# A 64-column product of zeros ahead of feed-forward stretches on TensorE

## The reference, cut to what matters

```
y = jnp.square(jax.nn.relu(h @ ff_w_in[layer])) @ ff_w_out[layer]      # layers 0 and 1: 1024 -> 4096 -> 1024
u, gate = jnp.split(h @ w_up, 2, axis=-1)                              # third: 1024 -> 2 x 2816
u = dwconv_grid(u, w_cf, b_cf, rows, width)
return (jax.nn.silu(u) * gate) @ w_down                                # 2816 -> 1024
```

## Time and profile before

| what | value |
|---|---|
| median of 3 runs | 1011.76 us (1010.94 to 1012.22) |
| the profiled execution, its own time | 1011.14 us |
| its span (first to last instruction) | 1009.2 us, so 1.9 us lie around it |
| TensorE matmuls, busy | 983.7 us, 97% of the span |
| TensorE weight loads, busy (beside the matmuls) | 865.8 us, 86% |
| VectorE, ScalarE, GpSimd busy | 801.6, 539.9, 77.4 us |
| DMA | 243.60 MB, mean 241 GB/s |
| mean granted TensorE clock | 0.996 of full speed |

### The profile page before, as it was taken

The page is one execution under the profiler, slowest core; times in us unless marked ns, Lnnn a source line. Parts: engine busy times, 40 slices in busy tenths (PEclk is TensorE's granted clock), DMA queues, the critical chain, the costliest instruction groups (busy, mean ns, idle before and its releaser), DMA issues.

```text
span 1009.2 us, 16926 instructions
## 1 busy us (share of the span) xinstructions
PE 983.7 (97%) x6900; PEld 865.8 (86%) x6901; DVE 801.6 (79%) x1208; ACT 539.9 (53%) x706; POOL 77.4 (8%) x80
## 2 busy tenths in 40 slices
PE   6999999999999999999999999999999999999997
PEld 3687799989987989887889999988998889999996
DVE  2449799858988988877979778873799789888896
ACT  4354554444446547775545455464765765454544
POOL 0000000000000000000540000000791000000000
PEclk9999999999999999999999999999999999999999
DMA  9999699969997999002998877735433386555511
GB/s 340 387 384 375 224 337 393 349 225 358 351 338 255 287 365 353 2 2 84 377 372 299 282 269 286 255 95 167 127 132 127 119 282 220 186 189 190 186 43 42
DMA packets 130332, 243.60 MB, mean 241 GB/s; under 512 B 6586, under 2 KB 95311, under 8 KB 124111
## 3 DMA queue, kind: packets, MB, share of 16 engines
q1 hardware_dynamic: 125616, 238.77, 66.9%
q10 hardware_dynamic: 4639, 3.76, 1.4%
HBM read 239.37 MB, written 1.05 MB: 238 GB/s over the span
## 4 chain that ended last, share of the span: by engine, by line
PE 76%; DVE 6%; DMA 5%; POOL 4%; ACT 4%; SPq 2%; issue 2%; POOLq 0%; DVEq 0%; ACTq 0%
PE bank L2039 26%; PE bank L1971 11%; PE bank L1973 11%; PE bank L1972 11%; PE bank L2051 3%; DMA raw<-in_a_w_in_dram 3%; DVE wlo L1199 2%; DMA raw<-in_cmp_w_dram 1%; PE bank L2324 1%; PE bank L2350 1%; SPq L654 1%; DMA raw<-in_b_w_in_dram 1%; ACT whi L724 1%; PE bank L1865 1%; PE bank L2362 1%
## 5 line engine op out<-in xcount | busy, mean ns | idle before, releaser
L1199 DVE TENSOR_TENSOR wlo<-raw,whi 128x2048 fp32r<-128x2048 f32 x143 | 327.3, 2295 | 47.3 <-ACT whi L724 46.2
L724 ACT ACTIVATE whi<-raw 128x2048 fp32r<-128x2048 f32 x144 | 274.3, 1905 | 144.6 <-PE bank L2039 76.6
L1971 PE MATMUL bank<-hcat,whi 128*128 128x256 f32 x1096 | 309.1, 282 | 2.3 <-DVE wlo L1199 1.9
L1972 PE MATMUL bank<-hcat,whi 128*128 128x256 f32 x1096 | 307.0, 280 | 0.0
L1973 PE MATMUL bank<-hcat,wlo 128*128 128x256 f32 x1096 | 306.9, 280 | 0.0
L1971 PEld LDWEIGHTS bank<-hcat,whi 128*128 128x128 f32 x1096 | 206.0, 188 | 9.1 <-issue 3.5
L1973 PEld LDWEIGHTS bank<-hcat,wlo 128*128 128x128 f32 x1096 | 208.9, 191 | 0.0
L1972 PEld LDWEIGHTS bank<-hcat,whi 128*128 128x128 f32 x1096 | 206.0, 188 | 1.4
L1818 DVE SCALAR_TENSOR_TENSOR cvt<-ut,vec,cvt 128x189 f32<-128x189 f32 (+2 forms) x176 | 68.2, 429 | 19.3 <-ACT cvt L1162 16.8
L2039 PE MATMUL bank<-whi,fhi 128*128 128x512 f32 x240 | 74.7, 392 | 0.0
L2039 PE MATMUL bank<-wlo,fhi 128*128 128x512 f32 x240 | 74.0, 390 | 0.0
(11 more groups left out here) (432 smaller groups left out, 1649.6 us busy)
## 6 DMA issues: line engine op xcount, KB each, us to landing
raw<-in_ada_w_dram SPq DMA_DIRECT2D x40, 1024.0 KB, 8.5
raw<-in_ff_w_in_dram SPq DMA_DIRECT2D x32, 1024.0 KB, 7.9
raw<-in_ff_w_out_dram SPq DMA_DIRECT2D x32, 1024.0 KB, 7.3
raw<-in_w_ada_dram SPq DMA_DIRECT2D x24, 1024.0 KB, 6.3
raw<-in_w_up_dram SPq DMA_DIRECT2D x22, 1024.0 KB, 5.1
raw<-in_w_in_dram SPq DMA_DIRECT2D x12, 1024.0 KB, 5.5
raw<-in_w_down_dram SPq DMA_DIRECT2D x11, 1024.0 KB, 4.9
raw<-in_ada_w_dram SPq DMA_DIRECT2D x16, 512.0 KB, 12.0
```

The lines of the kernel that those rows point to most:

```text
L724: act.activation(whi[:, m % SPL, 0:w], raw[:, pl.nm[m] % RAW, 0:w], ACT.Copy).then_inc(s_hi, 1)
L1199: dve.tensor_tensor(wlo[:, m % SPL, 0:w], raw[:, pl.nm[m] % RAW, 0:w], whi[:, m % SPL, 0:w], ALU.subtract).then_inc(s_lo, 1)
L1971: pe.matmul(dst, wh[:, kt, n], ah[:, kt, :], start=kt == 0, stop=False)
L1972: pe.matmul(dst, wh[:, kt, n], al[:, kt, :], start=False, stop=False)
```

## The change

A function `offset_start` issues one more matmul, of bf16 zeros: stationary `zb[:, 0:128]`, moving `zb[:, 0:64]`, into the first 64 columns of the bank that the stretch behind it writes, with `start` and `stop` set. The first product of the stretch begins with `start=True` too and so overwrites it. It is issued behind the waits of the stretch and ahead of its 48 products, for each `ff_in(c)` with c > 0 (15 in each of the first two layers) and for `up(M_UP[c + 1])` (10 in the third layer). `up(M_GA[...])`, which follows `up(M_UP[...])`, gets none, nor does any stretch outside of the feed-forward layers.

```diff
+KICK = 64
...
-            def feature_major(m, bank, ah, al, between=None):
+            def offset_start(bank):
+                pe.matmul(bank[:, 0:KICK], zb[:, 0:P], zb[:, 0:KICK], start=True, stop=True)
+
+            def feature_major(m, bank, ah, al, between=None, offset=False):
                 wh, wl = w_of(m)
+                if offset:
+                    offset_start(bank)
                 for nt in range(wh.shape[2] // P):
...
-            def linear_mid(m, ah, al, tm=False, o=None, between=None):
+            def linear_mid(m, ah, al, tm=False, o=None, between=None, offset=False):
...
-                    mm = feature_major(m, bank, ah, al, between)
+                    mm = feature_major(m, bank, ah, al, between, offset)
...
-                    linear_mid(m0 + (2 * c - 1 if c else 0), hh, hl, o=o)
+                    linear_mid(m0 + (2 * c - 1 if c else 0), hh, hl, o=o, offset=c > 0)
...
-                def up(m, bank, o=None):
+                def up(m, bank, o=None, offset=False):
                     split_ready(m)
                     if o is None:
-                        feature_major(m, ps[bank], hh, hl).then_inc(s_mm, 1)
+                        feature_major(m, ps[bank], hh, hl, offset=offset).then_inc(s_mm, 1)
...
-                        up(M_UP[c + 1], 6 + (c + 1) % 2)
+                        up(M_UP[c + 1], 6 + (c + 1) % 2, offset=True)
```

## The result

The changed kernel takes 1016.83 us in the median of 4 runs (1015.06 to 1018.0) against 1011.37 for the one before in the same session (1010.94 to 1012.22): a ratio of 1.0053, 95% interval 1.004 to 1.0066. It is slower. The profiled execution took 1015.06 us, the fastest of the four, with a span of 1013.2.

What follows compares the result with a forecast made beforehand. TensorE's matmul chain was taken as the bound. Pace gain 10.5 us, less 4.4 for kicks and 0.6 for settling, gives 5.5 less than the 1011.76 median: 1006.3 us, with an 8-in-10 range of 1004.8 to 1016.8.

Steps and rivals of the forecast that it cites:

- The bound: Feed-forward layers: TensorE's matmuls fill the windows, so the distance from one product to the next is their time.
- The two paces and their worth: Feature-major stretches of 48 products: 117.7 or 113.3 ns a product, 0.21 us a stretch, 10.5 us for 50 stretches.
- full flip: All 50 feed-forward stretches move to the fast pace: 5.5 us less after costs, 1006.3 us, chance 0.47.
- The no-flip rival: Kicked stretches stay at 117.7 ns, so the kicks are pure cost: 4.4 us more, 1016.2 us, chance 0.32.
- Whether it does: At the kicked stretches: whether the kick moves them to the fast pace, bounded by 0 and 10.5 us gained.
- The 17 pauses: Feature-major starts behind a pause of 0.15 us or more in the earlier trace: 14 fast, 3 slow.
- The six starts without a gap: Feature-major starts right behind short products, with no pause, in the earlier trace: all 6 slow.
- All or nothing: Kicked stretches: the same outcome expected nearly everywhere, because every 512-column run ends in the same steady rhythm.
- The price: On TensorE's chain, each kick costs a whole weight load, 0.11 us, 4.4 us for 40; bounds 1.1 to 5.2.
- the 229 ns a product of the rival: 512-column runs slow from 226.7 to 229 ns a product as the pace flips: 2.4 us lost, 1008.7, chance 0.06.
- Settling: At starts of fast stretches, a few slower products: some 0.016 us a start, 0.6 us for 40.
- The lower price: Kicks at the 25 ns issue floor: 1.0 us for 40, ending near 1002.9; cheaper kicks got chance 0.02.

Runs made afterwards that it cites:

- e13: Changed kernel with the last 512-column product of each run issued as 448 and 64 columns instead of a kick there, bf16 kick kept at five other places: 1005.16 us.
- e2: Changed kernel with each kick replaced by a TensorE wait for the end of its own earlier products: 1026.26 us, ratio 1.0136.
- e3: Changed kernel with a kick of 64 columns of real F32R operands, the stretch's first weights, instead of bf16 zeros: 1007.08 us, one run.
- e4: Changed kernel with the bf16 zero kick widened from 64 to 256 columns: 1006.72 us, one run.
- e8: Changed kernel with bf16 kicks of 256 columns behind the 512-column runs and 64 columns elsewhere: 1007.36 us, ratio 0.9955.
- e12: Changed kernel with two bf16 kicks of 64 columns in a row at each place: 1007.27 us, one run.
- e11: e3 with its real F32R kick at 128 columns instead of 64: 1014.89 us, one run.
- e14: e3 with its real F32R kick at 32 columns instead of 64: 1015.94 us, one run.
- e9: The changed kernel run and traced once more with nothing altered: 1016.06 us, ratio 1.0048.
- e1: Changed kernel with the zero kick moved from ahead of the 48 products to behind the first three, adding onto their sums: 1007.13 us, ratio 0.9953.
- e7: Changed kernel with the bf16 zero kick widened from 64 to 128 columns: 1015.12 us, one run.

## Why the prediction was wrong

**The bound** held: TensorE's chain fills the layers, and what the steps gain or lose comes out in the time. In e13 the steps of the 35 places (26 of them 0.100 us shorter, 9 by 0.314) make 5.4 us and the time fell by 5.9; in e2 they make 15.2 and it rose by 14.5.

**The two paces and their worth** held. 48 products take 5.44 or 5.65 us, and flipping them is worth 0.21 us: e3, e4, e8 and e12 have 36 to 40 of the 40 places fast. Against the kernel before of the same session they gain 4.7, 5.0, 4.5 and (with two kicks) 3.5 us, where the prediction's sum for a full flip has 5.5; the steps of e8 alone give 4.0 for the 35 places (26 x 0.060 + 9 x 0.273). The shortfall is the price, below. The no-flip rival had the time right too: 1016.2, measured 1016.83 and 1016.06.

**The step that failed is "Whether it does".** The prediction took the kick "as nearer to the pause, by the idle load path", and gave the flip 0.55 in all against 0.32. Both halves of that were wrong. The load path was not as pictured: the zeros' weights were loaded only as the kick started, not under the 512-column product. And where it was as pictured, with real F32R operands, it decided nothing: with the loads at the same moments e3 (64 columns) flips and e11 and e14 (128 and 32) don't. A pause, the thing it was likened to, frees nothing behind a 512-column run: e2 is slow at 35 of 35 places. The 17 pauses of the kernel before stood behind other work. Starts of that kind, moreover, change from one execution to the next (e9), so one trace's share of them was no firm chance. The six starts without a gap, all slow, gave the outcome that came, but they were no firm analogue either: one of them, behind transposes, was fast in the first trace of the changed kernel (e9). The range ended at 1016.8, 0.03 us short of the measured median. By the price of 0.12 that the text names for this end it would be 1016.6 (40 x 0.12 = 4.8), by its own highest price, 0.13, 1017.0.

**All or nothing** held behind the 512-column runs: in all runs that treat the 35 places alike, they all go one way. It was wrong for the rest: the 5 exceptions of the changed kernel, of which three go with the kick and two (behind a wait) came out both ways without one.

**The price** was mis-sized. The term was 0.11 us a kick; the load that follows comes 0.122 us late, as the kick's own load is no longer hidden, and the 512-column run behind pays 0.026 more, which the prediction had at 0. Together 0.147 at the 35 slow places, 5.1 us, where the prediction's 0.11 gives 3.9 for them. Had the pace stayed slow at all 40, it would be 5.9 in place of 4.4. The run behind the stretch pays in the fast cases too (5.455 to 5.458 us in e1, e3 and e4, from its first product to the kick or the next stretch, against 5.440); it never fell to the 229 ns a product of the rival. Settling, put at 0.016 us a start, measured 0.003 in e4 and 0.018 in e3.

The lower price that the prediction discarded has its place after all. The Trainium skill, page "TensorE: Matmul & The Clock Gate", section "Back-to-back issue gap", has a floor of 25 ns for a product of up to 64 columns. The trace comes near it where bf16 follows bf16, 0.03 us for the second kick of e12; where F32R weights must be loaded next it is 0.108 us, the same behind 32, 64 and 128 columns (e14, e3, e11).

The same page's section "Step-by-step: what each phase is for" says that loading the next weights takes no SBUF read bandwidth from the running product. The rival that leaned on it, only the price and no phase, is refuted by e3 and e13: the same 48 products with the same loads take 5.44 or 5.65 us. Whether reads have to do with it no run shows.

**What stays open** is the mechanism, and with it why 64 columns of zeros don't flip the pace and 64 real ones do. Behind a 512-column run, by the records (median of the 26 places in the first two layers, which differ by 1 or 2 ns), the second product's start behind its load was 0.117 us in e2, e11 and e14 and 0.119 in e7 and the changed kernel, all slow, and 0.122 to 0.125 in e3, e4 and e13, all fast, which would make a threshold; but e12 is fast with 0.118. Nor does the second product's distance from the last 512-column product order them: 0.455 us is slow (e11, e14), 0.460 fast (e3), 0.472 slow (e7, the changed kernel), 0.475 and 0.500 fast (e4, e12), 0.732 slow (e2). What in the chip holds either pace was not found, and no run measured a read conflict directly.

## What to carry to other kernels

Look for the same product at two distances before looking for fewer products: the median record length of one line, stretch by stretch, shows a 4% pace difference that no busy share does. To shift a stretch, try the last product ahead of it in two parts before adding one, and sweep the width of what you add: of real kicks 64 columns worked and 32 and 128 didn't, of bf16 kicks 256 and not 64 or 128. The product in two parts was tried with 448 and 64 alone. Price an added product by the weight load that must follow it, and check in the trace that its own load went under its predecessor, above all when its type differs.

## What was not expected of the hardware

- The bf16 weight load behind an F32R product was not pulled ahead in the changed kernel: it began 0.226 us after the start of a 512-column product and 0.118 after that of a 256-column one (at 831.2), with the kick itself, while F32R loads begin 0.003 us after it (e3). Behind the transposes, whose records are 0.27 us, it was pulled ahead and began 0.002 us after the last one's start. No run changed the type alone.
- The pace of 48 to 96 products is fixed within the first few, with starts that differ by as little as 3 ns. Behind a 512-column run it came out alike at all places with the same start, in every trace; behind pauses and transposes it changed from one execution of a kernel to the next.
- A pause of 0.31 us on TensorE behind a 512-column run didn't reset it (e2).
